# Turning queries and keys in the block of the product ahead, a norm by head pairs, and loads issued at once, in a two-block float32 transformer kernel

## The reference

```python
# per token and per pair of heads (128 columns)
o = o * rsqrt(mean(o * o, over the 128 columns) + 1e-6) * subln_gain * (1 - lambda_init)
y = o @ w_o
```

## Time and profile before

| | us |
|---|---|
| Median of three runs | 4065.89 |
| The profiled execution's own time | 4063.22 |
| Its span (all instructions) | 4061.4 |
| TensorE busy | 3768.1 |
| DVE busy | 1985.6 |
| ACT busy | 1332.0 |

### The profile page before, as it was taken

One profiled execution on the slowest core, in us unless ns is written; L12 is line 12 of the kernel. 1 busy time (PEld: TensorE's weight loads), 2 busy tenths in 40 slices (PEclk: granted clock), 3 DMA queues, 4 the chain that ended last, 5 costly groups with the idle time before them and its releaser, 6 DMA issues. The chain is left out here.

```text
span 4061.4 us, 54770 instructions
## 1 busy us (share of the span) xinstructions
PE 3768.1 (93%) x20683; PEld 3010.1 (74%) x20683; DVE 1985.6 (49%) x2914; ACT 1332.0 (33%) x2279; POOL 807.4 (20%) x604
## 2 busy tenths in 40 slices
PE   5988889999999899999998899999999988898998
PEld 3776578888877677777776688888878865577776
DVE  3736653333353375343436654333356737746444
ACT  3335532122143354222325422121224324433222
POOL 0500011212222121222220011212110018701222
PEclk9999999999999999999999999999999999999999
DMA  4124303323222221544310013323211140032221
GB/s 174 62 83 125 94 32 125 124 93 121 86 66 70 75 51 36 183 145 154 107 64 1 1 55 128 116 88 124 93 63 52 61 139 14 19 104 92 91 90 68
DMA packets 191734, 352.34 MB, mean 87 GB/s; under 512 B 41980, under 2 KB 43597, under 8 KB 191565
## 3 DMA queue, kind: packets, MB, share of 16 engines
q1 hardware_dynamic: 189277, 346.07, 25.9%
q10 hardware_dynamic: 2304, 4.20, 0.3%
HBM read 341.71 MB, written 16.92 MB: 88 GB/s over the span
## 5 line engine op out<-in xcount | busy, mean ns | idle before, releaser
L559 POOL TENSOR_TENSOR x<-x,scaled_buf 128x512 f32<-128x512 f32 (+1 forms) x360 | 466.8, 1302 | 2337.2 <-DVE scaled_buf L551 2336.9
L129 DVE TENSOR_TENSOR w_lo<-raw,w_hi 128x2048 fp32r<-128x2048 f32 x198 | 457.7, 2312 | 821.9 <-ACT w_hi L123 810.1
L123 ACT ACTIVATE w_hi<-raw 128x2048 fp32r<-128x2048 f32 x197 | 377.3, 1915 | 1223.6 <-PE psum L378 1221.2
L376 PE MATMUL psum<-hT_hi,w_hi 128*128 128x256 f32 (+1 forms) x1920 | 676.9, 353 | 3.3 <-DVE hT_lo L779 2.5
L377 PE MATMUL psum<-hT_lo,w_hi 128*128 128x256 f32 (+1 forms) x1920 | 673.5, 351 | 0.0
L378 PE MATMUL psum<-hT_hi,w_lo 128*128 128x256 f32 (+1 forms) x1920 | 673.4, 351 | 0.0
L376 PE MATMUL psum<-w_hi,uT_hi 128*128 128x512 f32 x1280 | 512.1, 400 | 17.1 <-DVE uT_lo L630 17.1
L551 DVE TENSOR_TENSOR scaled_buf<-psum,gate 128x512 f32<-128x512 f32 x360 | 246.9, 690 | 534.8 <-PE psum L378 530.0
L378 PE MATMUL psum<-w_hi,uT_lo 128*128 128x512 f32 x1280 | 506.0, 395 | 0.0
L377 PE MATMUL psum<-w_lo,uT_hi 128*128 128x512 f32 x1280 | 505.9, 395 | 0.0
L376 PE MATMUL psum<-w_hi,hT_hi 128*128 128x512 f32 x1072 | 419.6, 391 | 9.3 <-ACT qkv L1295 5.9
(11 more groups left out here) (276 smaller groups left out, 4762.8 us busy)
## 6 DMA issues: line engine op xcount, KB each, us to landing
mod_wide<-in_w_mod SPq DMA_DIRECT2D x24, 3072.0 KB, 10.5
raw<-in_w_mlp SPq DMA_DIRECT2D x64, 1024.0 KB, 5.2
raw<-in_ff_w SPq DMA_DIRECT2D x64, 1024.0 KB, 5.2
raw<-in_ssm_w_in SPq DMA_DIRECT2D x20, 1024.0 KB, 5.1
mod_slab<-in_w_mod SPq DMA_DIRECT2D x8, 2048.0 KB, 8.1
raw<-in_a_w_qkv SPq DMA_DIRECT2D x12, 1024.0 KB, 5.1
raw<-in_b_w_qkv SPq DMA_DIRECT2D x12, 1024.0 KB, 5.1
mod_first<-in_w_mod SPq DMA_DIRECT2D x4, 2048.0 KB, 16.3
```

Source lines behind the costliest of these rows:

```text
L123: act.activation(K.w_hi[h][:, :, :], K.raw[h][:, :, :], ACT.Copy).then_inc(K.hi_done.h, 1)
L129: dve.tensor_tensor(K.w_lo[h][:, :, :], K.raw[h][:, :, :], K.w_hi[h][:, :, :].bitcast(F32), ALU.subtract).then_inc(K.lo_done.h, 1)
L376: pe.matmul(out, hi_a, hi_w, start=first, stop=False, **check)
L559: pool.tensor_tensor(x, x, K.scaled_buf[:, j % 2, :], ALU.add).then_inc(K.added.h, 1)
```

## The change

It has five parts.

1. `clear_stage` moves into the block of `start_stage`. The large loads of the start (first block of `w_mod`, `x`, `ctx`, two more blocks, the first weight half, later the fourth block) are issued by ACT from its first instruction on; SP issues the small ones. Negating the bias table moves from DVE's first operation to behind the vectors' work.
2. The three `turn_stage`s move into the block of the product ahead of them. TensorE waits for the last evacuation there (and for the last rotary sum and gain), not for the block's end.
3. The split of the last weight half leaves the product's end: ACT does it behind item 4 of the turns, DVE behind item 7. The load of the half after it is issued by SP in `turn_stage`, there behind the other loads.
4. In the first attention ACT squares the output of unit v - 2 at the end of step v, with the sum over its 128 columns; the last two follow a load of the table for the root.
5. `head_norm_stage` goes. Its roots are one operation of ACT over 8 x 6 sums, its reciprocal one of DVE; DVE scales the output by pair over the six tiles, pairs 0 and 1 ahead of the splits and pair k + 2 behind the split of feature k. The gate's rows move into `operand_stage`.

```diff
 class Operand:
     def turn(self, K, pe, k):
+        if self.pairs is not None:
+            pe.wait_ge(K.normed.h, self.pairs.nr0 + k + 1)
...
     def lo_parts(dve):
...
                               ALU.subtract).then_inc(K.feat_lo.h, 1)
+            if pairs is not None and k + 2 < k_tiles:
+                pairs.pair(K, dve, k + 2)
...
+class PairNorm:
+    def roots(self, K, act):
+        act.preload_act_table(ACT.Sqrt)
+        act.wait_ge(K.sq_done.h, K.sq_done.n)
+        act.activation(K.pair_std[:, :, :], K.pair_ss[:, :, :], ACT.Sqrt, bias=K.eps6[:, 0:1], scale=1.0 / P).then_inc(K.std_done.h, 1)
+    def pair(self, K, dve, p):
+        if p == 0:
+            dve.wait_ge(K.std_done.h, self.sd0 + 1)
+            dve.reciprocal(K.pair_ss[:, :, :], K.pair_std[:, :, :]).then_inc(K.rstd_done.h, 1)
+            dve.wait_ge(K.rstd_done.h, self.rs0 + 1)
+        x = self.src[:, :, p * P:(p + 1) * P]
+        dve.tensor_tensor(x, x, K.pair_ss[:, p, :].unsqueeze(2).to_broadcast([P, TOK_TILES, P]), ALU.mult).then_inc(K.normed.h, 1)
+    def rest(self, K, dve):
+        self.pair(K, dve, 0)
+        self.pair(K, dve, 1)
...
 def start_stage(...):
         @block.scalar
         def _(act):
+            mod_block(0)
+            act.dma_start(K.x[:, 0:LAT_TILES, :], x.rearrange("(t p) n -> p t n", p=P)).then_inc(K.inputs_loaded.h, 16)
+            act.dma_start(K.x[:, LAT_TILES:TOK_TILES, :], ctx.rearrange("(t p) n -> p t n", p=P)).then_inc(K.inputs_loaded.h, 16)
+            mod_block(1)
+            mod_block(2)
+            load_half(K, act, 0, 0, first.half(0, 0), first=True)
             act.wait_ge(K.c_done.h, cn0 + 1)
             act.activation(K.cexp[:, :], K.vecs[:, 0:4 * KD], ACT.Exp, scale=-1.0).then_inc(K.c_done.h, 1)
...
+            act.wait_ge(K.mod_used.h, us0 + 1)
+            mod_block(3)
             act.wait_ge(K.inputs_loaded.h, 32)
+            act.wait_ge(K.cleared.h, 2)
             norm.roots(K, act)
...
 def turn_stage(...):
-    with K.nc.Block() as block:
+    with engines(K) as block:
...
             def _(sp):
+                sp.wait_ge(K.w_used.h, used)
+                sp.wait_ge(K.rotated.h, ro0)
+                sp.wait_ge(K.pool_chain.h, pc0)
                 for out, src in loads:
...
+                load_half(K, sp, *K.last_load)
                 sp.wait_ge(K.small_loaded.h, sm0 + 16 * len(loads))
...
         def _(pe):
+            pe.wait_ge(K.evacuated.h, ev0)
+            pe.wait_ge(K.rotated.h, ro0)
+            pe.wait_ge(K.pool_chain.h, pc0)
...
+                if i == 4:
+                    split_hi(K, act, g_held, 1)
...
+                if i == 7:
+                    split_lo(K, dve, g_held, 1)
...
 def attention_stage(..., squares=False):
+            def squared(v):
+                u = units[v]
+                act.wait_ge(K.o_read.h, at(K.o_read, v))
+                act.wait_ge(K.sq_done.h, sq0 + v)
+                act.activation(K.square_a[:, :], out(u.pair, u.tile), ACT.Square, accum_out=K.pair_ss[:, u.pair, u.tile:u.tile + 1])\
+                   .then_inc(K.sq_done.h, 1)
...
+                if squares and s >= 2:
+                    squared(s - 2)
...
+            if squares:
+                act.preload_act_table(ACT.Sqrt)
+                for v in range(N - 2, N):
+                    squared(v)
...
-        head_norm_stage(K, K.qkv, PAIRS, P, every, gate=2)
         with together(K):
-            operand_stage(K, qkv_at, KD, True, K.hT_hi, K.hT_lo, scale=lambda k, cls: K.sub_gain[:, 0:1])
+            operand_stage(K, qkv_at, KD, True, K.hT_hi, K.hT_lo, scale=lambda k, cls: K.sub_gain[:, 0:1], gate=2,
+                          norm=PairNorm(K, K.qkv), by_pairs=True)
```

More of the change, by code:

```diff
@@ L405, in ahead_loop, with gemm_stage @@
         body(n - 1, True, True)
[L409 removed]
+def gemm_stage(K, stream, nxt, k_tiles, tiles, evacuate, evac_on, hi_t=None, lo_t=None, hold=False, norm=None, affine=None, behind=None, turning=None,
+               before_turns=False):
     nc = K.nc
@@ L769, in operand_stage @@
     held, K.held = K.held, None
-    operand = Operand(K, src, k_tiles, classes, gate is not None)
+    pairs = norm if by_pairs else None
+    operand = Operand(K, src, k_tiles, classes, gate is not None, pairs)
     tr0, ft0, fh0, fl0, mm0 = (s.n for s in (K.turned, K.feat_done, K.feat_hi, K.feat_lo, K.mm_done))
@@ L835, in _ @@
             pe.wait_ge(K.mod_added.h, K.mod_added.n)
-            if norm is not None:
+            if norm is not None and pairs is None:
                 pe.wait_ge(K.normed.h, norm.nr0 + tiles)
@@ L893, in clear_stage @@
 def clear_stage(K):
-    nc = K.nc
-    with nc.Block() as block:
+    with engines(K) as block:
         @block.gpsimd
         def _(pool):
-            for s in K.credited:
-                pool.sem_inc(s.h, CREDIT)
+            pool.memset(K.rel_table[:, :, :], 0.0).then_inc(K.cleared.h, 1)
             pool.memset(K.eps6[:, :], NORM_EPS)
@@ L904, in _ @@
             pool.memset(K.eps_ln[:, :], LN_EPS / ALPHA ** 2)
-            pool.memset(K.one[:, :], 1.0)
-            pool.memset(K.rel_table[:, :, :], 0.0)
+            pool.memset(K.one[:, :], 1.0).then_inc(K.cleared.h, 1)
+            for s in K.credited:
+                pool.sem_inc(s.h, CREDIT)
 def start_stage(K, x, ctx, first, w_mod, groups, rpb, lambdas, norm):
@@ L1280, in root, with slab @@
                                scale=1.0 / HEAD_DIM).then_inc(K.std_done.h, 1)
+            def slab(p, n, held):
+                split_hi(K, act, st.g0 + n + 1, 0)
+                for j, t in enumerate(p.tiles):
+                    if j < p.nt - 1:
+                        act.wait_ge(K.mm_done.h, (n - p.n0) * (p.nt - 1) + (p.mm + j + 1))
+                    else:
+                        act.wait_ge(K.w_used.h, 2 * (st.g0 + n) + 2)
+                    if p.gain is not None:
+                        act.wait_ge(K.sums_done.h, (n - p.n0) * p.nt + (p.ss + j - 1))
+                        act.activation(K.slab_sq[:, j % 2, :], K.bank[j][:, :], ACT.Square).then_inc(K.sq_done.h, 1)
+                    act.activation(K.qkv[:, t, ds(n * SLAB_N, SLAB_N)], K.bank[j][:, :], ACT.Copy).then_inc(K.evacuated.h, 1)
+                    if p.gain is not None and j:
+                        root(p, n, j - 1)
+                if p.gain is not None:
+                    root(p, n, p.nt - 1)
+                if not held:
+                    split_hi(K, act, st.g0 + n + 1, 1)
@@ L1282, in _ @@
             act.preload_act_table(ACT.Sqrt)
             for p in parts:
-                with act.Fori(p.n0, p.n1) as n:
-                    split_hi(K, act, st.g0 + n + 1, 0)
-                    for j, t in enumerate(p.tiles):
-                        if j < p.nt - 1:
-                            act.wait_ge(K.mm_done.h, (n - p.n0) * (p.nt - 1) + (p.mm + j + 1))
-                        else:
-                            act.wait_ge(K.w_used.h, 2 * (st.g0 + n) + 2)
-                        if p.gain is not None:
-                            act.wait_ge(K.sums_done.h, (n - p.n0) * p.nt + (p.ss + j - 1))
-                            act.activation(K.slab_sq[:, j % 2, :], K.bank[j][:, :], ACT.Square).then_inc(K.sq_done.h, 1)
-                        act.activation(K.qkv[:, t, ds(n * SLAB_N, SLAB_N)], K.bank[j][:, :], ACT.Copy).then_inc(K.evacuated.h, 1)
-                        if p.gain is not None and j:
-                            root(p, n, j - 1)
-                    if p.gain is not None:
-                        root(p, n, p.nt - 1)
-                    split_hi(K, act, st.g0 + n + 1, 1)
+                held = p.n1 == stream.count
@@ L1302, in _ @@
+                with act.Fori(p.n0, p.n1 - held) as n:
+                    slab(p, n, False)
+                if held:
+                    slab(p, p.n1 - 1, True)
         @block.vector
@@ L1368, in heads_gemm_stage @@
     K.small_loaded.n += 16 * loads
+    K.held = st.g0 + stream.count
 class Turning:
@@ L1482, in turn_stage, with _ @@
     copied = len(items) - len(copies)
-    with K.nc.Block() as block:
-        if loads:
+    (g_held, K.held), used = (K.held, None), 2 * K.slabs
+    ev0, ro0, pc0 = K.evacuated.n, K.rotated.n, K.pool_chain.n
+    with engines(K) as block:
+        if not loads:
             @block.sync
             def _(sp):
+                load_half(K, sp, *K.last_load)
+        else:
+            @block.sync
+            def _(sp):
+                sp.wait_ge(K.w_used.h, used)
+                sp.wait_ge(K.rotated.h, ro0)
+                sp.wait_ge(K.pool_chain.h, pc0)
                 for out, src in loads:
@@ L1545, in turn_stage, with attention_stage @@
     K.src_read[1].n += len(items) // 2
-def attention_stage(K, units, q_of, k_of, values, out, diff=False, bias=False, sink=False, mod=None):
+def attention_stage(K, units, q_of, k_of, values, out, diff=False, bias=False, sink=False, mod=None, squares=False):
     nc = K.nc
```

226 lines of the change are left out of this document (76 added, 150 removed).

## The result

The changed kernel takes 4022.18 us (median; 4020.22 to 4023.76), the kernel before in the same comparison 4065.91: a ratio of 0.9894 with an interval of 0.9878 to 0.9909. That is 43.7 us less; the forecast was 36.2 less (4029.7). The profiled execution took 4022.81 us with a span of 4021.0, against 4061.4 before, so the traces account for 40.4. (The profiled execution of the kernel before lies 2.7 us under its median, that of the changed one 0.6 above.)

A forecast was written before the change was run, and what follows sets the result against it. TensorE, busy 93% of the span, bounds the kernel, so only its 293 us of idle can be won. Terms -11.5 - 6.1 - 6.5 - 6.3 - 7.8 + 2 = -36.2 us give 4029.7 against 4065.9; range 4020 to 4046.

The forecast's parts named there:

- kind bound: The favourable end of a term's bounds, for the second turns -8.3 us against the term's -6.5; together they gave 4020.
- The start, -11.5: Kernel start: the load stream begins earlier, input turns at 50.4 instead of 61.9 us; bounds -14 and 0.
- ACT issues at about 7.6: Kernel start: ACT's first load issue at about 7.6 us, with the stream taken to start at 10.0.
- ScalarE's slack: Kernel start: ACT's issues done 16.3 us into the stream, ACT free at 26, with 2 to 4 us of slack.
- the rival of a start without gain: Kernel start: ACT's queue or late small vectors keep the fourth product at 55 us; total 4041, chance 0.13.
- Three turn stages, -6.1, -6.5, -6.3: First, second and third turns: TensorE or the bias loads start earlier, saving 6.1, 6.5 and 6.3 us.
- The norm, -7.8: Between first attention and output product: product starts earlier, -9.5 us less 1.7 for slow clock; bounds -5 and -10.
- The chain of -9.5: At the norm: cast, difference and scaling, 2.45 us a feature, let the product begin at 511.85 instead of 521.35.
- the slow clock: At the norm: idle among the turns may start the output product at 1.2 GHz, taken as 1.7 us lost.
- Squares, +2: First attention: 48 squares of 0.5 us, 24 us of ACT work, mostly in its waits; +2 us, bounds 0 and 24.
- the rival of the attention's chain: First attention: the squares delay ACT's copies that release TensorE, adding 24 us instead of 2; total 4052, chance 0.10.
- The table: First attention: rival that square and exponential need different tables, 48 x 2 loads of 1.28 us; total 4151, chance 0.02.

The follow-up runs named there:

- The experiment with the clearing apart: Changed kernel with GpSimd's clearing again in a block of its own, counts first, ahead of the start's block: 4029.84 us.
- the start alone: Kernel before with only the new start (clearing inside the first block, large loads issued by ScalarE): 4047.27 us against 4064.94, ratio 0.9958.
- the run with three: Changed kernel with every square of the first attention made three times, one behind the other: 4025.67 us.
- the eight pairs: Changed kernel with all eight pairs of heads normalised ahead of the first turn instead of two ahead of the first cast: 4022.12 us.
- the one mask: Changed kernel with only the second pair's bias mask moved from the turn stage into the second attention's block: 4020.67 us.
- the combined kernel: Changed kernel with four pairs ahead, second pair's mask in the attention, first weights behind the fourth modulation block, their low part behind the scale: 4011.79 us.

## Why the prediction was right, and where not

The direction, the likeliest case and the range held (4022.2 in 4020 to 4046), near the lower end. The miss is 7.5 us. By the traces the terms together came to -46.0 instead of -36.2, with 4.2 of the difference at the start and 3.0 at the squares; some of it was given back later, in part by the clock, and that this brought the total nearer to the forecast is luck. (The bounds were added with 1.5 for the second turns, whose kind bound lies 1.8 under the term; that moves the lower end by 0.3.)

- **The start, -11.5, measured -15.7: mis-sized, and beyond its own bound of -14.** The step that failed is "ACT issues at about 7.6". The earlier trace rows show GpSimd's memset at 7.63, and I took that time for the engines' own readiness. It was the seven microseconds in which GpSimd counted semaphores before it, inside the block that held everyone. The change puts the counts behind the memsets and all in one block: first issue at 0.75. With 2.3 us from issue to the full stream and 33.5 to the fourth product, the sum would have been 36.6; it came at 39.96, 3.4 later. By an estimate from the DMA view, with 390 GB/s as full, the four slices with 194 to 309 GB/s cost 1.9 us and the thin end from 37.2 on about 2. So an error of 6.9 was partly covered by one of 3.4 the other way. The experiment with the clearing apart shows the first of the two; the second is read from the DMA view alone.
- **ScalarE's slack.** It was free at 22.5, inside the 26 that the prediction allowed, but only because the stream began 7 us before its time: counted from there the issues took 19.4 us, not 16.3. The fourth product still waited for its load alone, and the rival of a start without gain (0.13) is out.
- **Three turn stages, -6.1, -6.5, -6.3: measured -6.4, -7.5, -6.6** (from the product's last matmul to the attention). The sizes are right, the fast clock from the first turn too. The reason was told as two savings and is one: the deferred split and the joined block each remove it nearly alone. In the second stage the bias landed 7.05 us after its issue instead of 9.3 (9.4 in the start alone, which has the old order; 7.0 to 7.6 in all kernels with the new one where the mask waits for nothing else), so the megabyte that was moved behind it had cost about 2.3 us and not the 0.9 that I took.
- **The norm, -7.8, measured -8.8.** The chain of -9.5 came to the tenth; the slow clock cost 0.7, not 1.7. What the prediction did not see is that the work by pairs, whose splitting it priced step by step, adds nothing to this.
- **Squares, +2, measured -1.0 for the attention as a whole.** The direction of the earlier trace rows was read rightly: idle ahead of copies took the squares in. But that idle fell to 60.3 us and not to 47, since 48 squares made ScalarE 12.6 us busier and not 24. The -1.0 goes with the clock: 13.7 us of this attention at the lower level against 17.1. The rival of the attention's chain (0.10) is out by the run with three.
- **The table.** No load stands among the units: ScalarE's only one in 268 to 476 us is the written preload of the root's table ahead of the last two squares (L1738). That agrees with the earlier trace rows; the Trainium skill, ScalarE: Activation LUTs, "Table sets: the hidden batching unit", does not name the square in its list of sets, and its price of a switch was not needed.
- **Given back.** At the first matmul of the third attention the changed kernel is 45.5 us ahead, at the end of the span 40.4. The third attention gave back 1.4 us, the stretch from its last matmul to the program's last one 4.6 (1713.4 us, the kernel before 1708.8), and what stands behind that one took 1.0 less. The 4.6 are no effect of the change: all these kernels have the same code there, six of them took 1708.8 to 1709.1, among them four that differ from the changed kernel in one place only, far ahead of this stretch; the others took up to 1713.6 (the eight pairs 1713.4, the one mask 1713.5) and down to 1707.4. Two short stretches hold 2.9 us of it: 80 matmuls from 3487.3 us on took 18.6 us at a granted clock of 0.86, in the kernel before 16.8 at 0.98, and 14 from 3652.0 on took 4.3 us at 0.66, before 3.2 at 1.00.

## What to carry to other kernels

A stall at a block's end has several parents, and removing any one of them may free it all: price the pair and not the sum, and try each alone. The time of an engine's first instruction is no proof that it could not have begun earlier; look for what its queue did before, and for who waited at the same barrier. Work that is cut into portions helps only if the portions that the next engine needs first are the ones made first; here four in advance gained 3.5 to 5 us over two, and two gained nothing over eight.

## What was not expected of the hardware

- Counting is not free: GpSimd's 82 semaphore counts took 6.7 us, 0.08 each, ahead of its memsets, in a stretch that the timeline shows as 7.07 us of idle.
- An engine that issues large DMAs can stand still in the issue: ScalarE 12.10 us for two blocks of 2 MB and 7.88 for a half of 1 MB, with its exponential behind them. With the half's issue moved, the first modulation product began 8.55 us earlier.
- An addition of 128x2 on VectorE took 2.33 us while GpSimd masked 128x2048 in the same block, and 0.16 in the changed kernel at the same place, where the masks were done. It ended at 1343.28, and the two masks, one row of 8.96 us from 1334.29 on, at 1343.25. In the combined kernel it took 1.86 us and ended with its mask too (1339.56 and 1339.54). It is the same at every later mask of this attention: in the changed kernel six such additions took 1.09 to 1.49 us, in the kernel before six took 1.15 to 1.67, and each ended 0.02 us after its mask. The custom operations, the reduction and the copies out of PSUM beside the same masks were not longer. So in these traces this addition never ended while GpSimd's operation ran; the cause was not tried by itself.
- The same code at the end of the first attention ran at either clock: the gate's 32 matmuls took 3.81 us in some kernels' executions and 5.3 in others, after attentions whose last twelve matmuls had 1.58 or 2.90 us (with three squares 1.58, and yet 5.43 for the gate's). It decides over 2.3 us (24.36 against 26.7), more than several of the edits here.
